# Layer-1 mLSTM mixer: the sample tile processed third of five, with its states and spread buffers in their own memory

## What is computed

```python
q, k, v, o, i_pre, f_pre = split_last(x @ w_in, MLSTM_SIZES)   # 8 heads, qk 64, v 128
ig = soft_cap(i_pre + b_i); lf = log_sigmoid(soft_cap(f_pre + b_f))
# per chunk, for every sequence and head:
b = cumsum(fc); d = where(causal, b_t - b_j + i_j, -inf); g = b + m
mt = max(g, d.max(-1)); w_inter = exp(g - mt)
att = exp(d - mt) * (q @ k.T)
num = w_inter * (C @ q) + att @ v;  den = w_inter * (n . q) + att.sum(-1)
h = num / max(abs(den), exp(-mt))
C = dec * C + sum_j w_state_j v_j k_j;  n = dec * n + sum_j w_state_j k_j
# then
h = rms_norm(h, mh_norm); out = (h * sigmoid(o)) @ w_out
x = layer_norm(ALPHA * x + out)
```

## Time and profile before

| | us |
|---|---|
| median of 3 runs | 4361.26 (4354.4 to 4364.62) |
| span of the profiled execution | 4359.5 |
| mLSTM block in it | 2480.5 to 2984.4 (504) |
| of it tiles 0 to 3, to the cumulation of tile 4 | 2480.5 to 2835.4 |
| of it the sample tile | 2835.4 to 2984.4 (149) |
| TensorE busy over the span | 3848.5 (88%) |
| VectorE busy over the span | 2764.4 (63%) |

### The profile page before, as it was taken

The page is one execution under the profiler, slowest core; times in us unless marked ns, Lnnn a source line. Parts: engine busy times, 40 slices in busy tenths (PEclk is TensorE's granted clock), DMA queues, the critical chain, the costliest instruction groups (busy, mean ns, idle before and its releaser), DMA issues. The chain is left out here.

```text
span 4359.5 us, 50665 instructions
## 1 busy us (share of the span) xinstructions
PE 3848.5 (88%) x17166; PEld 2860.4 (66%) x17166; DVE 2764.4 (63%) x6184; ACT 1006.0 (23%) x2810; POOL 1544.8 (35%) x1332
## 2 busy tenths in 40 slices
PE   9798958888899989989898789977999899898986
PEld 4477844445777767777676545555777777676765
DVE  0255632222599987877776623335999888877777
ACT  0132201121122255431010112211222455310000
POOL 0011213332035365555554200000263655655553
PEclk9888979899999989999999899968999999899998
DMA  3100056775568799999999674404598999999996
GB/s 129 43 15 17 27 161 186 206 205 165 191 247 335 299 400 417 416 410 379 392 395 389 249 255 167 154 19 156 215 343 309 371 416 417 404 387 392 389 398 257
DMA packets 374218, 1168.40 MB, mean 268 GB/s; under 512 B 36914, under 2 KB 163523, under 8 KB 345994
## 3 DMA queue, kind: packets, MB, share of 16 engines
q0 software_dynamic: 159920, 570.80, 34.3%
q1 hardware_dynamic: 187386, 518.08, 32.7%
q10 hardware_dynamic: 26656, 76.29, 4.6%
HBM read 1091.93 MB, written 68.59 MB: 266 GB/s over the span
## 5 line engine op out<-in xcount | busy, mean ns | idle before, releaser
L2046 POOL DMA_INDIRECT peer_ru<-in_u_rows,peer_expert x512 | 797.8, 1558 | 1697.1 <-DVE peer_expert L2426 831.5
L2124 PE MATMUL peer_bank<-peer_xT,peer_u 128*128 128x288 f32 x4096 | 1032.4, 409 | 1.8 <-ACT peer_held L2251 1.8
L2124 PEld LDWEIGHTS peer_bank<-peer_xT,peer_u 128*128 128x128 f32 x4096 | 775.2, 192 | 208.0 <-issue 3.4
L2345 DVE SCALAR_TENSOR_TENSOR y<-peer_rv,peer_weight,y 128x1024 f32<-128x1024 f32 x512 | 656.4, 1282 | 80.2 <-issue 56.5
L2355 DVE CUSTOM_DVE_ANT_0 peer_ru<-peer_ru,x 128x1024 f32<-128x1024 f32 x512 | 623.2, 1217 | 40.7 <-DMA peer_ru<-in_u_rows,peer_expert 40.1
L2054 POOL DMA_INDIRECT peer_rv<-in_v_rows,peer_expert x512 | 536.0, 1047 | 234.2 <-issue 143.6
L2175 PE MATMUL peer_bank<-peer_u,region 128*128 128x288 f32 x1664 | 428.9, 421 | 62.8 <-DMA region<-in_v 62.8
L2175 PEld LDWEIGHTS peer_bank<-peer_u,region 128*128 128x128 f32 x1664 | 328.1, 198 | 161.0 <-DMA region<-in_v 67.4
L2175 PE MATMUL peer_bank<-region,peer_u 128*128 128x288 f32 x1536 | 376.4, 406 | 0.0
L2197 ACT ACTIVATE peer_act_g<-peer_dot 128x1 f32<-128x1 f32 x512 | 103.6, 202 | 1152.9 <-DVE peer_dot L2355 1143.2
L2494 DVE TENSOR_TENSOR peer_hidden<-peer_hidden,peer_bank 128x288 f32<-128x288 f32 x496 | 220.7, 451 | 228.0 <-PE peer_bank L2175 226.5
(11 more groups left out here) (519 smaller groups left out, 4982.2 us busy)
## 6 DMA issues: line engine op xcount, KB each, us to landing
peer_u<-in_uT SPq DMA_DIRECT2D x128, 1024.0 KB, 8.5
peer_u<-in_v SPq DMA_DIRECT2D x32, 2048.0 KB, 12.6
region<-in_v SPq DMA_DIRECT2D x32, 2048.0 KB, 14.2
mlstm_w_in<-in_w_in_o SPq DMA_DIRECT2D x30, 1792.0 KB, 7.3
mla_keys<-in_keysT SPq DMA_DIRECT2D x256, 144.0 KB, 4.8
mla_vals<-in_cache_ckv POOLq DMA_DIRECT2D x256, 128.0 KB, 5.2
peer_held<-in_wq SPq DMA_DIRECT2D x16, 2048.0 KB, 8.4
scratch_early<-peer_hidden ACTq DMA_DIRECT2D x50, 576.0 KB, 9.5
```

The costliest lines, as they stand in the source:

```text
L2046: pool.indirect_dma_start(ru[:, n % U_ROWS, :], None, u_rows, bass.IndirectOffsetOnAxis(ap=expert[:, T, k:k + 1], axis=0)).then_inc(ru_in[ ...
L2124: mm = mmul(bank[:, UNIT_BANKS[i], 0:TD], u[:, h % URING, i % 2, k, :], xT[:, k, :], start=k == 0, stop=k == KD - 1)
L2345: V.scalar_tensor_tensor(out=y[:, T, :], in0=rv[:, n % V_ROWS, :], scalar=weight[:, n:n + 1], in1=y[:, T, :], op0=ALU.mult, op1=ALU.add).t ...
```

## The change

The order of the tiles becomes 0, 1, sample, 2, 3 (`TILE_AT`, with `SPOS` = 2 the position of the sample tile); everything that indexes rows of `x` or `xT` goes through that table. `Ss` gets its own memory and is loaded by SyncE ahead of the weight slots from 9 on, behind the output weights. A second spread buffer stands beside `big` (`apart`). The numerators use the banks 3, 4, 5 and 0 instead of 3, 4, 5 and 7. The decay rows (`dsel`) are made before the numerators and spread right behind them. The state products of pair p follow the projection chunk 4+p of the next tile (chunks 4, 5, 6, then none); pair p waits until the numerators are out of their banks (p = 0) or until the sums of pair p-1 are done (`ss_ok`). On VectorE the spread of the keys and the sums of the pairs are put between the steps that the tile has anyway. The next `cumulate` waits for all four sums. The stores of the sample's states come after that, the prompt's at the very end.

```diff
+    TILE_AT = [0, 1, SAMP, 2, 3]
+    SPOS = TILE_AT.index(SAMP)
...
-        Ss = ring[:, 0:NB * PAIRS * VA].rearrange("p (b q x) -> p b q x", b=NB, q=PAIRS)
+        Ss = sb("Ss", [P, NB, PAIRS, VA])
+        apart = [sb("apart", [P, NSEG, P]), big]
...
-        SNUM, SST = ((4, 3), (5, 7)), (1, 2, 6, 0)
+        SNUM, SST = ((4, 3), (5, 0)), ((1, 0, 3), (2, 3, 6), (0, 6, 8))
+        state_at = lambda b: next((at, (b - lo) * VA) for at, lo, hi in SST if lo <= b < hi)
+        stp_before = lambda n: n + (PAIRS - 1 if n > SPOS else 0)
...
                 sp.dma_start(w_out[:, :, :], A["w_out_o"].rearrange("(k p) n -> p k n", p=P)).then_inc(out_in, 16)
                 sp.dma_start(gain[:, :], A["ln1_g1"].partition_broadcast(P)).then_inc(out_in, 16)
                 sp.dma_start(shift[:, :], A["ln1_b1"].partition_broadcast(P)).then_inc(out_in, 16)
+                sp.dma_start(Ss[:, :, :, :], A["cn_s"]).then_inc(ss_in, 16)
                 for s in range(NOC + 2, NOC * TILES):
                     load_w(s)
-                sp.wait_ge(fill_mm, FILL_AT["p", NOC * TILES - 1] + 1)
-                sp.dma_start(Ss, A["cn_s"]).then_inc(ss_in, 16)
...
+                sp.wait_ge(m_ok, SPOS + 1)
+                sp.dma_start(O["m_s"], m_s[:, :]).then_inc(outs, 16)
+                sp.wait_ge(ss_ok, PAIRS)
+                sp.dma_start(O["cn_s"], Ss[:, :, :, :]).then_inc(outs, 16)
+                sp.wait_ge(m_ok, TILES)
+                sp.dma_start(O["m_p"], m_p[:, :]).then_inc(outs, 16)
+                sp.wait_ge(num_kept, TILES)
                 for g in range(2):
                     half = slice(g * 64, (g + 1) * 64)
                     sp.dma_start(O["cn_p"][half], Sz[half, :, :].rearrange("p (q g) x -> p q g x", g=2)[:, :, g, :]).then_inc(outs, 16)
...
-                    pe.wait_ge(fill_kept["v"], FILL_COUNT[FILL_AT["o", 2 * SAMP - 1]])
                     for h in range(H):
                         p, half = h // 2, slice(h % 2 * 64, h % 2 * 64 + 64)
                         if h % 2 == 0:
                             pe.wait_ge(spread, p + 1)
                         mmul(hbs(h), attT[:, h, :], va[:, h, :], start=True, stop=False)
                         for b in range(NB):
-                            mm = mmul(hbs(h), big[half, b, :], Ss[half, b, p, :], start=False, stop=b == NB - 1)
+                            mm = mmul(hbs(h), apart[p % 2][half, b, :], Ss[half, b, p, :], start=False, stop=b == NB - 1)
                         if h % 2:
                             mm.then_inc(spread_used, 1)
-
-                def sample_states():
                     pe.wait_ge(dsel_ok, 1)
-                    mmul(bank[:, 0, 64:64 + NB * H], C["ones"], dsel[:, :, :].rearrange("p a b -> p (a b)"), start=True, stop=True).then_inc(dcol, 1)
...
+                    mmul(bank[:, 0, 320:320 + NB * H], C["ones"], dsel[:, :, :].rearrange("p a b -> p (a b)"), start=True, stop=True).then_inc(dcol, 1)
+
+                def sample_states(t, p):
+                    pe.wait_ge(spread, PAIRS + p + 1)
+                    if p == 0:
+                        pe.wait_ge(num_kept, t + 1)
+                    else:
+                        pe.wait_ge(ss_ok, p)
+                    for g in range(2):
+                        for b in range(NB):
+                            at, col = state_at(b)
+                            mm = mmul(bank[g * 64:(g + 1) * 64, at, col:col + VA], apart[p % 2][:, b, g * 64:(g + 1) * 64], va[:, 2 * p + g, :],
+                                      start=True, stop=True)
+                    mm.then_inc(stp, 1)
...
+                    if t == SPOS:
+                        sample_numerators(t)
+                        for p in range(PAIRS):
+                            if p < NOC - 4:
+                                fill("p", NOC * (t + 1) + 4 + p)
+                            sample_states(t, p)
+                    else:
                         numerators(t)
-                        for c in range(4, NOC):
-                            fill("p", NOC * (t + 1) + c)
+                        if ahead:
+                            for c in range(4, NOC):
+                                fill("p", NOC * (t + 1) + c)
+                    if ahead:
+                        if t == SPOS:
+                            pe.wait_ge(ss_ok, PAIRS)
                         cumulate(t + 1)
-                    else:
-                        sample_numerators(t)
-                        sample_states()
-                pe.wait_ge(ss_ok, 1)
...
+                def spread_keys(p):
+                    tt(apart[p % 2][:, :, :], mid(kw[:, p * P:(p + 1) * P], NSEG), last(C["seg_of_row"], P), ALU.mult).then_inc(spread, 1)
+                    for g in range(2):
+                        half = slice(g * 64, (g + 1) * 64)
+                        ins = tt(Ss[half, :, p, :], Ss[half, :, p, :], dec[half, :, 2 * p + g:2 * p + g + 1].to_broadcast([64, NB, VA]), ALU.mult)
+                    ch(ins)
+
+                def add_states(t, p):
+                    dve.wait_ge(stp, stp_before(t) + p + 1)
+                    for at, lo, hi in SST:
+                        s4 = Ss[:, lo:hi, p, :]
+                        ins = tt(s4, s4, bank[:, at, 0:(hi - lo) * VA].rearrange("p (c x) -> p c x", x=VA), ALU.add)
+                    ins.then_inc(ss_ok, 1)
...
                     if not one:
+                        tt(dsel[:, :, :], mid(ex[:, 3, :], NB), last(C["newest"], H), ALU.mult).then_inc(dsel_ok, 1)
                         dve.wait_ge(att_tk, 3 * (t + 1))
                         for p in range(PAIRS):
-                            if p:
-                                dve.wait_ge(spread_used, p)
-                            tt(big[:, :, :], mid(qpT[:, p, :], NSEG), C["seg_of_col"].rearrange("p (c x) -> p c x", x=P), ALU.mult).then_inc(spread, 1)
+                            if p >= 2:
+                                dve.wait_ge(spread_used, p - 1)
+                            tt(apart[p % 2][:, :, :], mid(qpT[:, p, :], NSEG), C["seg_of_col"].rearrange("p (c x) -> p c x", x=P), ALU.mult).then_inc(spread, 1)
                         norm_factors(t - 1)
+                        dve.wait_ge(dcol, 1)
+                        ch(V.tensor_copy(flat(dec[:, :, :]), bank[:, 0, 320:320 + NB * H]))
                         dve.wait_ge(spread_used, PAIRS)
-                        tt(dsel[:, :, :], mid(ex[:, 3, :], NB), last(C["newest"], H), ALU.mult).then_inc(dsel_ok, 1)
-                        dve.wait_ge(dcol, 1)
-                        ch(V.tensor_copy(flat(dec[:, :, :]), bank[:, 0, 64:64 + NB * H]))
-                        for p in range(PAIRS):
-                            tt(big[:, :, :], mid(kw[:, p * P:(p + 1) * P], NSEG), last(C["seg_of_row"], P), ALU.mult).then_inc(spread, 1)
...
-                            dve.wait_ge(stp, SAMP + p + 1)
...
                     else:
-                        dve.wait_ge(num, t + 1)
-                        dve.wait_ge(stp, t + 1)
+                        dve.wait_ge(num, t + 1 - (t > SPOS))
+                        dve.wait_ge(stp, stp_before(t) + 1)
...
+                    if not one:
+                        spread_keys(0)
+                        spread_keys(1)
                     if one and t:
                         norm_factors(t - 1)
                     ch(tt(attT[:, :, :], Em[:, :, :], Em[:, :, :], ALU.mult))
                     ch(V.tensor_reduce(ms[:, 0, :], attT[:, :, :], AX, ALU.add))
                     tsc(ms[:, 1, :], ms[:, 0, :], 1.0 / DV, 1e-6, ALU.mult, ALU.add).then_inc(ms_ok, 1)
+                    if not one:
+                        add_states(t, 0)
+                        spread_keys(2)
                     if ahead:
                         gates(t + 1)
                     if t:
                         norm_end(t - 1)
+                    if not one:
+                        add_states(t, 1)
+                        spread_keys(3)
                     dve.wait_ge(root, t + 1)
                     ch(V.reciprocal(ms[:, 0, :], ms[:, 2, :]))
                     ch(tt(Em[:, :, :], Em[:, :, :], last(ms[:, 0, :], DV), ALU.mult))
...
                         dve.wait_ge(fill_kept["a"], FILL_COUNT[FILL_AT["t", 2 * t - 1]])
                     tt(mix[:, :], flat(Em[:, :, :]), row(t)[:, 2 * AW + H * DV:2 * AW + 2 * H * DV], ALU.mult).then_inc(mix_ok, 1)
                     dve.wait_ge(mix_ok, t + 1)
+                    if not one:
+                        add_states(t, 2)
+                        add_states(t, 3)
                     if ahead:
                         begin(t + 1)
```

More of the change, by code:

```diff
@@ L2685, in cumulate @@
                     pe.wait_ge(exq, t)
[L2686 removed]
+                    mmul(bank[:, 0, 0:H], C["upto" if t != SPOS else "upto16"], lfs[:, :], start=True, stop=True).then_inc(cum, 1)
                 def spread_e(t):
@@ L2940, in _ @@
                 for t in range(TILES):
-                    one, ahead = t < SAMP, t + 1 < TILES
```

(1 more changed line is left out.)

49 lines of the change are left out of this document (12 added, 37 removed).

## The result

| | before | after |
|---|---|---|
| median | 4354.4 us (7 runs, 4341.1 to 4364.6) | 4326.3 us (7 runs, 4313.1 to 4337.8) |
| ratio, 95% interval | | 0.9934 (0.9912 to 0.9955) |
| span of the profiled execution | 4359.5 | 4315.4 |
| mLSTM block in it | 2480.5 to 2984.4 (503.9) | 2459.8 to 2939.3 (479.5) |
| of it, last cumulation to the end | 149.0 | 81.4 |

The kernel became 28 us faster (20 to 38 by the interval). The forecast of 4338 us lies 12 us above the median, and the lower end of the range, 4328, lies 2 us above it.

A forecast was written before the change was run, and what follows sets the result against it. Prompt tiles run at TensorE's pace; in the sample tile neither TensorE nor VectorE is full. New end -68.4, middle +40.1, load +5.4 sum to -22.9 us; from 4361.3 that gives 4338 us, range 4328 to 4360 (forecast's own 4331 to 4346).

The forecast's parts named there:

- The new end: Last cumulation to block end, now in a prompt tile: 80.6 us against 149.0, a gain of 68.4 us.
- The middle: Sample tile, numerators' start to next cumulation: 69.0 us against a prompt tile's 28.9, a loss of 40.1 us.
- The wait ahead of states 2: TensorE, before pair 2's state products in the sample tile: idle 9.4 us until VectorE's sum of pair 1.
- The rival with everything hidden: All state updates hidden between chunks: middle 54 us, total -38 us or 4323 us; chance 0.04.
- The clock in the numerators: Sample numerators, straight behind chunk 3: run at clock 1.00 and take 17.2 us, bounds 17.2 and 36.
- low clock rival: Sample numerators at low clock take 36 us, chunk 4 1.6 more: +20.4 us, 4359 us in all; chance 0.15.
- The load: Sample states' load in SyncE's queue ahead of weight slot 9: costs 5.4 us, between 0 and 6.3.
- The slot's wait: TensorE's wait for weight slot 9, behind the states' load: near 15 us instead of 9.7.
- The block: The whole mLSTM block: -22.9 us, 480 us instead of 504.
- the tile behind the sample tile: The tile after the sample tile was taken as a normal one, with no gain or loss.
- the last of the sum: Whole kernel's time: span 4359.5 us plus 1.8 to the runs' median, 4361.3, less 22.9, gives 4338 us.
- The next mixer: The stage behind the block, its code unchanged: the forecast is wrong if it takes another time.

The follow-up runs named there:

- e3: The changed kernel with VectorE adding pair 1 and spreading the keys of pair 3 ahead of the gates; ratio 0.9943 to the kernel before, block 477.4 us.
- e4: e3 with the sum of pair 2 straight behind the gates and that of pair 3 behind norm_end; ratio 0.9929 to the kernel before, block 468.5 us.
- e12: The changed kernel with three more spreads of pair 0 on VectorE ahead of the sample numerators; block 486.0 us, one run.
- e8: The changed kernel with five more spreads of pair 0 on VectorE ahead of the sample numerators; ratio 0.9994 to the kernel before, block 505.9 us.
- e10: The changed kernel with one spread buffer instead of two, later key spreads behind the previous pair's sum; ratio 0.9994 to the kernel before, block 499.9 us.
- e2: The changed kernel run again, unchanged; ratio 0.9947 to the kernel before, block 478.7 us.
- e9: e8 with chunk 4 put between the wait and the sample numerators instead of behind them; ratio 0.9980 to the kernel before, block 493.0 us.

## Why the prediction was right in the block and wrong in the time

- **The new end**: 81.4 us, forecast 80.6; the numerators start 35.6 us behind the cumulation (2893.40; forecast 36.0). Right.
- **The middle**: 69.1 us from the numerators to the cumulation, forecast 69.0. That it is so close is partly luck, since its parts were off by small amounts that cancel: a head took 2.40 us instead of 2.15, the numerators so 19.1 instead of 17.2 (the head's own terms, 1.7, 0.22 and 0.2, give 17.0), and states 2 took 6.23 instead of 5.7; the change from one step to the next cost a little less than was set. The wait ahead of states 2 is 9.20 (forecast 9.4), its cause confirmed by e3 and e4. The rival with everything hidden had 54 us for this stretch; e4, which hides all but short waits, took 55.0.
- **The clock in the numerators**: right by its condition, that they come straight behind chunk 3 and no pair waits. The first spread is done 2.1 us ahead of them, and a wait of 1.66 us on top did no harm (e12), one of 4.17 did (e8), nor may a pair wait inside them (e10). The prediction read the 3.75 us of idle TensorE ahead of the old numerators as a low entry; they too began at 1.00 and fell within the first head. The price of the low clock rival, +20.4, is near: the numerators and chunk 4 of e8 cost 17.4 us more (15.8 and 1.6), with the waits it is 21 to 23 in the sample tile.
- **The load**: 4.8 us in the mean of the profiles, forecast 5.4. The slot's wait is 12.9 to 15.1 us where near 15 was forecast.
- **The block**: forecast -22.9; 24.4 in the first pair of profiles, 25.5 in the mean of two each. By stretches of the table: the end -67.7 (forecast -68.4), the middle +40.0 (+40.1), the first two tiles with the load +3.2 (+5.4), and the tile behind the sample tile -1.1, which was put at nothing. It starts behind a wait of 1.45 us instead of 4.33, and its turns and first chunk took 1.07 and 5.54 us in the changed kernel where tile 2 of before had 1.90 and 6.44.
- **The step that failed is the last of the sum**, the level from which the 22.9 us were taken. I took the median of three runs, 4361.3, for the level of the kernel before and "runs that lie 5 us around their median" for their spread. The seven runs beside those of the changed kernel have a median of 4354.4, and with that the same sum gives 4331.5, inside the range; 77 later runs of the same kernel have a median of 4351.0, and single ones lie between 4335 and 4371. So the level was 7 to 10 us too high, and the spread three times as wide. On 4351 the sum gives 4328, where the changed kernel's 16 runs (seven, and nine in e2) have a median of 4330. The 5 us that are left between 4331.5 and the seven runs' 4326.3 are 2.6 from the block and otherwise no more than such medians scatter: the nine of e2 gave 4332.0. A range around the same forecast with that scatter of 15 us to either side would have held the median.

The next mixer, named as what would prove the forecast wrong if it took another time, took the same within the scatter of all kernels here.

## What to carry to other kernels

When a serial tail is moved between other work, most of its gain can be lost to the order in which another engine makes what the moved steps need: look at what each step waits for, and put the sums that TensorE needs next ahead of gates and norms that nobody waits for yet (here 14 us for moving four calls). Moving one of them only moves the wait on to the next. The numerators here, a run of matmuls with 64 rows, want to begin close behind full ones and have their operands ready ahead: the double buffer was worth the clock of the whole run, not the 1.3 us of each wait, and without that clock the move is a loss.
For the forecast: a term of 25 us on a kernel whose runs lie 35 us apart is read in the stage, and the level of the time needs more than three runs, or a range that holds their spread.

## What the runs showed of the hardware that was not expected

- Matmuls with 64 rows ran at granted clock 1.00 over 19.1 us straight behind a chunk, and behind 1.66 us of idle TensorE too (e12). Behind 4.17 us they began at 1.00, fell to 0.50 within the first head and stayed there over 34.8 us of unbroken work (e8). A chunk with 128 rows in the same place brought the clock back within 8 us (e9), and products with 128 rows, 64 columns and the numerators' width within 6.2 (states 2).
- An idle time of 1.32 us inside such a run dropped the clock, within that idle time, for the 29.6 us that were left of the run (e10).
- The start of the block, counted from the first instruction and behind the same code, lay between 2456.9 and 2484.4 us in thirteen profiles, and went with the mean granted clock of the first 1100 us (0.89 to 0.91).
